# One hybrid encoder layer: where the sums of x1 are formed, when PSUM is emptied, and when the last phase's weights are loaded

## The reference

```python
proj = x @ w_in                                   # q, k, v, gates, ...
ya = forgetting_attention(...) @ w_a_out
yb = gated_linear_attention(...) @ w_b_out
merged = sigmoid(ga) * ya + sigmoid(gb) * yb
x1 = LN(ALPHA * x + merged @ w_o)
up = x1 @ w_up                                    # 1024 -> 2 * 2816
conv = conv_b + sum(conv_w[j] * ext[:, j:j + T] for j in range(3))
val, gate = split(conv)
x2 = LN(ALPHA * x1 + (val * gelu(gate)) @ w_down)
e = (p @ w_pl) * sigmoid(x2 @ w_plg)
y = LN(ALPHA * x2 + e)
```

## Time and profile before

| | |
|---|---|
| median of 3 runs | 2327.8 us (2327.62 to 2330.48) |
| profiled execution, own time | 2328.35 us |
| its span | 2326.2 us |
| PE busy | 2236.5 us, 96% of the span |
| DVE, ACT, POOL busy | 51%, 34%, 20% |
| moved by transfers | 219.37 MB, mean 94 GB/s |
| mean granted TensorE clock | 0.987 |

### The profile page before, as it was taken

The page is one execution under the profiler, slowest core; times in us unless marked ns, Lnnn a source line. Parts: engine busy times, 40 slices in busy tenths (PEclk is TensorE's granted clock), DMA queues, the critical chain, the costliest instruction groups (busy, mean ns, idle before and its releaser), DMA issues.

```text
span 2326.2 us, 33184 instructions
## 1 busy us (share of the span) xinstructions
PE 2236.5 (96%) x13679; PEld 2066.2 (89%) x13679; DVE 1192.5 (51%) x1638; ACT 796.8 (34%) x1211; POOL 460.6 (20%) x545
## 2 busy tenths in 40 slices
PE   8999999999999999999999977999999998999997
PEld 8997677898989899999998877999999987888886
DVE  2226663263636363102434586766666655556446
ACT  3124664333333333113221124443444435333311
POOL 0001222001010101000031254454444510001011
PEclk9999999999999999999999998999999999999999
DMA  5109653202121212213214111222222257435420
GB/s 163 41 21 245 169 150 118 76 19 70 45 72 42 75 40 77 86 37 113 60 64 154 59 51 48 77 73 72 73 72 83 72 192 250 152 123 175 145 80 37
DMA packets 200907, 219.37 MB, mean 94 GB/s; under 512 B 40426, under 2 KB 161494, under 8 KB 200102
## 3 DMA queue, kind: packets, MB, share of 16 engines
q1 hardware_dynamic: 191750, 187.38, 26.5%
q0 software_dynamic: 9008, 29.87, 4.0%
HBM read 163.03 MB, written 41.53 MB: 88 GB/s over the span
## 4 chain that ended last, share of the span: by engine, by line
PE 85%; DVE 5%; SPq 2%; issue 2%; DMA 2%; ACT 2%; POOL 1%; DVEq 0%; ACTq 0%; POOLq 0%
PE ps L681 39%; PE ps L1150 19%; PE ps L1181 10%; PE ps L1229 4%; PE ps L1094 3%; PE ps L1005 2%; PE ps L860 1%; SPq L2929 1%; DMA down_raw<-in_w_down 1%; DVE sb L1850 1%; PE ps L820 1%; PE ps L713 1%; DVE sb L1954 0%; PE ps L842 0%; PE ps L1056 0%
## 5 line engine op out<-in xcount | busy, mean ns | idle before, releaser
L681 PE MATMUL ps<-x_hi,ring_hi 128*128 128x384 f32 x960 | 327.6, 341 | 0.5 <-ACT sb L1284 0.5
L681 PE MATMUL ps<-x_lo,ring_hi 128*128 128x384 f32 x960 | 322.1, 335 | 0.0
L681 PE MATMUL ps<-x_hi,ring_lo 128*128 128x384 f32 x960 | 322.0, 335 | 0.0
L1284 ACT ACTIVATE sb<-ps 18x256 f32<-18x256 f32 (+9 forms) x230 | 104.5, 475 | 352.9 <-PE ps L681 215.0
L1864 DVE TENSOR_TENSOR ring_lo<-ring_raw,ring_hi 128x1024 fp32r<-128x1024 f32 (+1 forms) x66 | 76.1, 1158 | 212.5 <-ACT ring_hi L1284 211.5
L681 PEld LDWEIGHTS ps<-x_hi,ring_hi 128*128 128x128 f32 x960 | 181.2, 189 | 4.0 <-issue 3.7
L681 PEld LDWEIGHTS ps<-x_lo,ring_hi 128*128 128x128 f32 x960 | 181.0, 189 | 0.9 <-issue 0.7
L681 PEld LDWEIGHTS ps<-x_hi,ring_lo 128*128 128x128 f32 x960 | 180.9, 188 | 0.0
L1181 PE MATMUL ps<-down_hi,h_hi 128*128 128x512 f32 x396 | 156.4, 395 | 12.5 <-DVE h_lo L2438 12.4
L1181 PE MATMUL ps<-down_hi,h_lo 128*128 128x512 f32 x396 | 155.0, 391 | 0.0
L1181 PE MATMUL ps<-down_lo,h_hi 128*128 128x512 f32 x396 | 154.8, 391 | 0.0
(11 more groups left out here) (352 smaller groups left out, 5713.1 us busy)
## 6 DMA issues: line engine op xcount, KB each, us to landing
down_raw<-in_w_down SPq DMA_DIRECT2D x66, 512.0 KB, 3.6
ring_raw<-in_w_in SPq DMA_DIRECT2D x50, 512.0 KB, 3.9
h_raw<-h_chunks SPq DMA_DIRECT2D x66, 192.0 KB, 3.7
sb<-in_x_prompt SPq DMA_DIRECT2D x24, 512.0 KB, 8.0
h_chunks<-convolved_halves SPq DMA_DIRECT2D x22, 512.0 KB, 2.8
up_raw_b<-in_w_up SPq DMA_DIRECT2D x42, 256.0 KB, 3.8
up_raw<-in_w_up SPq DMA_DIRECT2D x32, 256.0 KB, 3.0
branch_b<-sb POOLq DMA_DIRECT2D x4, 1152.0 KB, 7.2
```

The costliest lines, as they stand in the source:

```text
L681: m = mm(out, l, r, start=(n == 0), stop=(n == len(pairs) - 1))
L1284: return act.activation(out, in_, ACT.Copy, scale=scale)
```

## The change

1. DVE makes all sums of x1. The four POOL operations go; DVE makes S3 (three operations) behind `sum_lo(1)`, and the last addition of S4 behind `quarter_lo(1, T3)`. S4's first operation stays where it was. The semaphore `s_s4` goes.
2. On ACT, `first_out(1, 1)`, both `first_samples_out` and `keep_p1(1)` come ahead of later roundings: the order was `sum_hi(0)`, `sum_hi(1)`, `first_out(1, 1)`, samples, `sum_hi(2)`, `keep_p1(1)`, and becomes `sum_hi(0)`, `first_out(1, 1)`, samples, `sum_hi(1)`, `keep_p1(1)`, `sum_hi(2)`.
3. On SP, what step 0 issued is spread: `w_pl` at step 2, `w_plg` in eight pieces of 512 KB at steps 3 to 10, one gain or bias at each of steps 11 to 14. What step 4 issued comes at step 15. `embedding_hi` and `embedding_lo` move from steps 6 to 15 to the ten steps of `EMBEDDING_AT`, and wait for all four pieces of their half of `w_plg`.

```diff
+        EMBEDDING_AT = {s: j for j, s in enumerate((6, 7, 9, 10, 11, 12, 14, 15, 16, 17))}
...
             first_out(0, 1)
             sum_hi(0)
-            sum_hi(1)
             first_out(1, 1)
             first_samples_out(0)
             first_samples_out(1)
+            sum_hi(1)
+            keep_p1(1)
             sum_hi(2)
-            keep_p1(1)
             for i in (T3, T1, T4, B22):
                 quarter_hi(1, i)
...
-                act.wait_ge(s_xt[7 + c], 64)
+                act.wait_ge(s_xt[7 + c], 112)
...
-                if 6 <= s < 16:
-                    embedding_hi(s - 6)
+                if s in EMBEDDING_AT:
+                    embedding_hi(EMBEDDING_AT[s])
...
                 quarter_lo(1, T2)
                 quarter_lo(1, B21)
                 dve.wait_ge(s_x1s, 16 * NT)
-                dve.tensor_tensor(s4, h12, s2, ALU.subtract).then_inc(s_s4, 1)
-                dve.wait_ge(s_s4, 1)
+                link(dve.tensor_tensor(s4, h12, s2, ALU.subtract))
+                sum_lo(1)
+                link(dve.tensor_tensor(sum_r[2], h11, h21, ALU.subtract))
+                link(dve.tensor_tensor(sum_r[2], sum_r[2], l11, ALU.add))
+                dve.tensor_tensor(sum_r[2], sum_r[2], l21, ALU.subtract).then_inc(s_sp, 1)
+                dve.wait_ge(s_sp, 1)
+                quarter_lo(1, T3)
+                dve.tensor_tensor(s4, s4, x1l[:, 4:8, 0:HALF].bitcast(F32), ALU.add).then_inc(s_sp, 1)
...
             quarter_lo(1, B11)
             sums()
-            sum_lo(1)
-            quarter_lo(1, T3)
             sum_lo(2)
             add_u1(1)
...
-            pool.tensor_tensor(sum_r[2], h11, h21, ALU.subtract).then_inc(s_pool, 1)
-            pool.wait_ge(s_pool, 4)
-            pool.tensor_tensor(sum_r[2], sum_r[2], l11, ALU.add).then_inc(s_pool, 1)
-            pool.wait_ge(s_pool, 5)
-            pool.tensor_tensor(sum_r[2], sum_r[2], l21, ALU.subtract).then_inc(s_sp, 1)
-            pool.wait_ge(s_s4, 1)
-            pool.tensor_tensor(sum_r[3], sum_r[3], x1l[:, 4:8, 0:HALF].bitcast(F32), ALU.add).then_inc(s_sp, 1)
...
-                if s == 0:
+                if s == 2:
                     sp.dma_start(rpl, w_pl[0]...).then_inc(s_xt[6], 16)
-                    for c in range(2):
-                        sp.dma_start(rplg[c], w_plg[0]...[:, :, c * 512:(c + 1) * 512]).then_inc(s_xt[7 + c], 16)
-                    for v, dst in ((ln2_g, g2), (ln2_b, b2), (ln3_g, g3), (ln3_b, b3)):
-                        bcast(v[0], dst, s_g1)
+                if 3 <= s < 11:
+                    c, k = (s - 3) // 4, (s - 3) % 4 * 2
+                    sp.dma_start(rplg[c][:, k:k + 2, :], w_plg[0]...[:, k:k + 2, c * 512:(c + 1) * 512]).then_inc(s_xt[7 + c], 16)
+                if 11 <= s < 15:
+                    bcast((ln2_g, ln2_b, ln3_g, ln3_b)[s - 11][0], (g2, b2, g3, b3)[s - 11], s_g1)
                 if s == 1:
                     store_h(LAST)
-                if s == 4:
+                if s == 15:
                     sp.wait_ge(s_hs, 32 * NC_FF)
                     sp.wait_ge(s_cg, 2 * NC_FF)
                     ...                    # x1_in, p_in, as before
```

More of the change, by code:

```diff
@@ L619, in build @@
         s_sh, s_su = sem("x1_sum_hi_ready"), sem("x1_sum_lo_ready")
-        s_s4 = sem("x1_sum_begun")
         s_x1s = sem("x1_stored")
@@ L2358, in _, with sum_lo @@
             x1_lo(NT - 1)
+            def sum_lo(i):
+                dve.wait_ge(s_sh, 1 + i)
+                dve.tensor_tensor(sum_l[i], sum_r[i], sum_h[i].bitcast(F32), ALU.subtract).then_inc(s_su, 1)
             def sums():
@@ L2378, in sums @@
                 dve.wait_ge(s_x1s, 16 * NT)
-                dve.tensor_tensor(s4, h12, s2, ALU.subtract).then_inc(s_s4, 1)
-                dve.wait_ge(s_s4, 1)
-            def sum_lo(i):
-                dve.wait_ge(s_sh, 1 + i)
-                dve.tensor_tensor(sum_l[i], sum_r[i], sum_h[i].bitcast(F32), ALU.subtract).then_inc(s_su, 1)
+                link(dve.tensor_tensor(s4, h12, s2, ALU.subtract))
[6 more added lines that the diff above has]
+                dve.tensor_tensor(s4, s4, x1l[:, 4:8, 0:HALF].bitcast(F32), ALU.add).then_inc(s_sp, 1)
             def banks(o):
@@ L2567, in _ @@
                     dve.wait_ge(s_g1, 32 + 64)
-                if 6 <= s < 16:
-                    embedding_lo(s - 6)
+                if s in EMBEDDING_AT:
+                    embedding_lo(EMBEDDING_AT[s])
                 for what, *args in EVENTS.get(s - 1, ()):
@@ L2823, in _ @@
             copied(pool, *[("x1T", n) for n in range(NT)])
-            h11, l11, h21, l21 = (a[:, 0:4, c:c + HALF].bitcast(F32) for c in (0, HALF) for a in (x1h, x1l))
-            pool.tensor_tensor(sum_r[2], h11, h21, ALU.subtract).then_inc(s_pool, 1)
-            pool.wait_ge(s_pool, 4)
-            pool.tensor_tensor(sum_r[2], sum_r[2], l11, ALU.add).then_inc(s_pool, 1)
-            pool.wait_ge(s_pool, 5)
-            pool.tensor_tensor(sum_r[2], sum_r[2], l21, ALU.subtract).then_inc(s_sp, 1)
-            pool.wait_ge(s_s4, 1)
-            pool.tensor_tensor(sum_r[3], sum_r[3], x1l[:, 4:8, 0:HALF].bitcast(F32), ALU.add).then_inc(s_sp, 1)
             for c in range(1, NC_FF + 1):
@@ L3093, in _ @@
                     down_in(s + 4)
-                if s == 0:
+                if s == 2:
                     sp.dma_start(rpl, w_pl[0].rearrange("(k p) n -> p k n", p=P)).then_inc(s_xt[6], 16)
-                    for c in range(2):
-                        sp.dma_start(rplg[c], w_plg[0].rearrange("(k p) n -> p k n", p=P)[:, :, c * 512:(c + 1) * 512])\
-                            .then_inc(s_xt[7 + c], 16)
-                    for v, dst in ((ln2_g, g2), (ln2_b, b2), (ln3_g, g3), (ln3_b, b3)):
-                        bcast(v[0], dst, s_g1)
+                if 3 <= s < 11:
+                    c, k = (s - 3) // 4, (s - 3) % 4 * 2
+                    sp.dma_start(rplg[c][:, k:k + 2, :], w_plg[0].rearrange("(k p) n -> p k n", p=P)[:, k:k + 2, c * 512:(c + 1) * 512])\
+                        .then_inc(s_xt[7 + c], 16)
+                if 11 <= s < 15:
+                    bcast((ln2_g, ln2_b, ln3_g, ln3_b)[s - 11][0], (g2, b2, g3, b3)[s - 11], s_g1)
                 if s == 1:
                     store_h(LAST)
-                if s == 4:
+                if s == 15:
                     sp.wait_ge(s_hs, 32 * NC_FF)
```

## The result

| | before | after |
|---|---|---|
| median, in the same session | 2327.71 us (4 runs, 2326.75 to 2330.48) | 2307.94 us (4 runs, 2307.52 to 2309.35) |
| ratio, 95% interval | | 0.9914 [0.9897, 0.9931] |
| profiled execution, own time / span | 2328.35 / 2326.2 us | 2307.52 / 2305.7 us |
| PE busy | 2236.5 us, 96% | 2235.9 us, 97% |

What follows compares the result with a forecast made beforehand. PE, at 96% of the span, bounds the kernel, so only its waits can be won back: 2328.35 - 4.4 (sums) - 12.4 (load wait) - 1.4 (slow clock) = 2310.15, stated as 2310 us, range 2306 to 2316.

Steps and rivals of the forecast that it cites:

- Rival 2: First phase: DVE is slow for a reason of its own, taps start 7.9 us late, 2322.4 us; chance 0.08.
- One reading beside the sum: First phase: from 1385.93 on, POOL is done and each DVE operation takes 2.56 us.
- The sum by steps: First phase: DVE's sums of x1 timed one by one, taps start at 1414.15 instead of 1418.54, gaining 4.4 us.
- the balance at its end: First phase: DVE takes on 10.2 us that POOL carried; freedom from POOL gives back 13.2 us.
- the first added wait: First phase: `sum_lo(1)` waits for `sum_hi(1)`, now behind the samples; costs 0.8 us.
- The order of PSUM: First phase: emptying earlier removes PE's 14.1 us wait, but the gap moves to T3, about 10 us; counted at 0.
- 12.4 us of stall: Second phase, step 5: PE's wait for the late `down_in(5)` load goes, gaining 12.4 us.
- 1.4 us of slow clock: Second phase, after the gap before 1926: PE's clock, granted 0.63 for 4 us, stays full, gaining 1.4 us.
- rival 1: Second phase: burst at step 15 or step 2's load delays a `w_down` load, 2 to 8 us; chance 0.13.
- issued 4.09 us later: Second phase, step 15's burst: next step's load issues 4.09 us later, lands after 7.9 to 9.5 us, against 9.4.
- Rival 4: Second phase, steps 3 to 14: pieces land one after another, 10.8 us per step, total 2381 us; chance 0.03.
- the cover: Second phase: each step's 1.25 MB of loads takes 3.1 to 3.7 us, hidden inside its 4.09 us.

Runs made afterwards that it cites:

- experiments 5 and 6: Changed kernel with S3's three operations back on POOL: 2309.27 us; changed kernel with eight POOL fills beside DVE's S1 and S2: 2306.76 us (one run).
- experiment 9: Changed kernel with `w_plg` loaded in two pieces of 2 MB at steps 3 and 7 instead of eight of 512 KB: 2308.95 us, 0.9923.

## Why the prediction was right

**The sums.** The prediction's times, counted from B11 (1366.96 there, 1364.33 in the profile after):

| us after B11 | foretold | measured |
|---|---|---|
| S1 done | 8.3 | 8.35 |
| S2 done | 13.5 | 13.54 |
| wait before `sum_lo(1)` | 0.8 | 0.68 |
| low part of T3 starts | 31.1 | 30.98 |
| wait before it | 2.65 | 2.76 |
| T4 starts | 40.4 | 40.27 |
| taps start | 47.2 | 47.04 |

4.54 us instead of 4.4. The durations all came from rows in which POOL stood still, and experiments 5 and 6 show that this was the right reading. Rival 2 is out. One reading beside the sum is incomplete: POOL was not done at 1385.93, since its fourth operation ran from 1397.55 and T3's low part took 2.91 us behind it. The sum by steps has that low part at its undisturbed length and so holds the gain; the balance at its end (10.2 us of cost, 13.2 back) does not, and comes to 4.4 only with these 2.2 us and the 0.8 us of the first added wait: 13.2 - 10.2 + 2.2 - 0.8.

**The order of PSUM.** Counted at 0; alone 1.0001. The gap moved to T3, 10.14 us against "about 10".

**The loads.** 12.4 us of stall and 1.4 us of slow clock make 13.8; measured 13.20 in the profile pair, and 13.2 to 14.0 with the spans of 419.29 to 420.07 us that the other profiles with the spread loads show from step 0 on. So both terms hold within that scatter. The 0.6 us at step 20 is rival 1, at the place named for it, at a price below the 2 to 8 us given there; it was counted at 0, and was 0 to 0.6 us from profile to profile. The step that was a little off is "issued 4.09 us later": the load was issued 6.2 us after its forerunner, since SP was busy with the burst. Rival 4 is out, with PE at 4.08 us a step under 0.87 to 0.96 of queue time. That is 3.5 to 3.9 us of a step, where 3.1 to 3.7 were foretold: the cover was thinner than the sum had it, and held. The smaller pieces' rate, of which the prediction feared starved steps, cost some 4% (experiment 9).

**The 2.63 us ahead of B11** were not in the sum. B11 starts between 1363.60 and 1366.96 us in the 14 profiles of before, after and the experiments, whose programs agree up to there in what they compute; the changed kernel alone shows 1364.33 and 1365.54. The three profiles with the old sums have 1363.77, 1365.71 and 1366.96, the other eleven 1363.60 to 1366.58, so the line goes by execution and not by the change, and the kernel before happened to have the latest of all. So the profile pair overstates the change. Without this line it is 17.9 us; by the medians the changed kernel is 18.4 us faster against 2326.29 (18.2 foretold). The first pair of medians has 19.8, from 2327.71 for the kernel before, whose later medians are 2325.69 to 2326.30: the 2 us by which the forecast of 2310 was too high fit this scatter, and no term of the sum is off by as much. What makes the earlier phases scatter was not tried.

## What to carry to other kernels

A wait on the busiest engine is worth only as much as the chain that it stands in: cutting the 14.1 us wait to 8.9 gained nothing here, while each microsecond off the chain up to the taps was kept, though PE's list gave it no line of its own. Before an operation is moved to an idle engine, look at what it does to its neighbour; and before bulk loads are put between timed ones, count the issuing engine's own time as well as the bytes. When two profiles differ, cut both at landmarks first: what lies ahead of the edited place is not the change's.

## What the runs showed of the hardware that I had not expected

- POOL's and DVE's adds of 128x2304 elements take turns, a whole operation at a time: 7.51 and 7.33 us instead of 2.56 on DVE, while POOL's own three took 5.17, 5.49 and 7.28 us, the last of which ended 4.95 us after DVE's turn. Eight fills of the same size took 16.61 us, 2.08 each, and cost DVE nothing.
- The issue of one transfer, mostly 0.33 to 0.64 us in the second phase, took 4.87, 7.28 and 8.33 us (a load issued at 1913.17 in the kernel before) when several MB stood ahead of it; in the changed kernel the longest single issue from step 0 to step 15 took 1.88 us.
- The same 144 products took 19.42 or 20.95 us in two kernels that differ only later; the granted clock was 1.00 (2.4 GHz throughout) and 0.93 (a mean of 1.2 and 2.4 GHz) in that stretch. PE had been busy for 12.81 and 11.91 of the 16 us ahead of it; whether that difference is the cause was not tried.
